# Column halves for two groups of narrow matmuls, and another order of VectorE's work in a chunk loop

## The reference, cut to what matters

```python
# prompt attention, per head and block of 128 queries, causal
sc = einsum('bqhd,bkhd->bhqk', qn, k_nope) + einsum('bqhr,bkr->bhqk', qr, k_rope)
pr = softmax(where(kpos <= qpos, sc * MLA_SCALE, -inf))
o  = einsum('bhqk,bkhd->bqhd', pr, v)                       # v has 64 columns a head

# norms: sums of squares
o_mla = rmsnorm(o_mla, g_mla_out);  m = rmsnorm(mem, g_mem_kv)
kk = kk / max(sqrt(sum(kk * kk, -1)), 1e-12)                # per head of 64

# RWKV7 recurrence, per head, state S of 64 x 64
sa = -einsum('bhvk,bhk->bhv', S, kk_t)
S  = S * d_t + sa[..., None] * (kk_t * a_t) + v_t[..., None] * k_t
y  = einsum('bhvk,bhk->bhv', S, r_t)
```

## Time and profile before

| what | us |
|---|---|
| median of 3 runs | 2296.93 (2292.48 to 3044.49) |
| profiled execution | 2297.73 |
| its span, first to last instruction | 2296.1 |
| projection | 0 to 283 |
| prompt attention | 283 to 525 |
| sample attention | 525 to 655 |
| preparation | 655 to 771 |
| chunk loop, first chunk from 771 | 771 to 1010 |
| samples' chunk | 1010 to 1085 |
| output, memory attention, feed-forward | 1085 to 2296 |

### The profile page before, as it was taken

One profiled execution on the slowest core, in us unless ns is written; L12 is line 12 of the kernel. 1 busy time (PEld: TensorE's weight loads), 2 busy tenths in 40 slices (PEclk: granted clock), 3 DMA queues, 4 the chain that ended last, 5 costly groups with the idle time before them and its releaser, 6 DMA issues. The chain is left out here.

```text
span 2296.1 us, 51205 instructions
## 1 busy us (share of the span) xinstructions
PE 2140.7 (93%) x20986; PEld 1979.9 (86%) x20986; DVE 1331.1 (58%) x2648; ACT 664.4 (29%) x1349; POOL 118.2 (5%) x194
## 2 busy tenths in 40 slices
PE   7999999997979788889999999899999999999997
PEld 6999777776769688887899879899999999999997
DVE  6356565653445456654852364366666666666676
ACT  5120244443342445541231242231122111221121
POOL 0000000004400111110000000000000000000000
PEclk9999999998978999999999999999999999999998
DMA  4111100006723100023021351111111101111112
GB/s 159 47 44 41 48 7 12 12 1 161 187 83 103 35 4 4 4 71 94 28 79 37 113 199 47 34 56 43 45 52 55 44 31 47 47 56 47 32 49 76
DMA packets 81830, 134.03 MB, mean 58 GB/s; under 512 B 27186, under 2 KB 57779, under 8 KB 81491
## 3 DMA queue, kind: packets, MB, share of 16 engines
q1 hardware_dynamic: 70482, 119.22, 16.0%
q0 software_dynamic: 4224, 8.13, 1.4%
q10 hardware_dynamic: 6912, 3.54, 0.6%
HBM read 121.58 MB, written 9.29 MB: 57 GB/s over the span
## 5 line engine op out<-in xcount | busy, mean ns | idle before, releaser
L280 PE MATMUL psum<-high,ff_up 128*128 128x352 f32 x2112 | 517.5, 326 | 7.1 <-DVE ff_up L3048 4.5
L280 PEld LDWEIGHTS psum<-high,ff_up 128*128 128x128 f32 x2112 | 371.0, 189 | 8.7 <-DVE ff_up L3048 5.2
L280 PE MATMUL psum<-low,ff_up 128*128 128x352 f32 x1056 | 341.6, 323 | 0.0
L443 PE MATMUL psum<-h_high,pj_part 128*128 128x352 f32 x960 | 242.1, 330 | 15.0 <-DVE h_low L550 14.9
L280 PE MATMUL psum<-hid,ff_down 128*128 128x352 f32 x1440 | 234.4, 324 | 0.8 <-DVE x L3109 0.8
L280 PEld LDWEIGHTS psum<-hid,ff_down 128*128 128x128 f32 x1440 | 232.8, 188 | 1.1 <-DVE x L3109 1.1
L280 PEld LDWEIGHTS psum<-low,ff_up 128*128 128x128 f32 x1056 | 199.7, 189 | 0.0
L3109 DVE TENSOR_TENSOR x<-x,psum 128x352 f32<-128x352 f32 x264 | 136.4, 521 | 105.5 <-PE psum L280 105.2
L443 PEld LDWEIGHTS psum<-h_high,pj_part 128*128 128x128 f32 x960 | 171.7, 191 | 20.6 <-issue 10.7
L2954 ACT ACTIVATE ff_up<-ff_slot 128x1024 fp32r<-128x1024 f32 x46 | 48.3, 1050 | 393.1 <-PE psum L280 384.7
L443 PE MATMUL psum<-h_low,pj_part 128*128 128x352 f32 x480 | 157.2, 328 | 0.0
(11 more groups left out here) (443 smaller groups left out, 4210.2 us busy)
## 6 DMA issues: line engine op xcount, KB each, us to landing
ff_slot<-in_w_up SPq DMA_DIRECT2D x44, 512.0 KB, 3.6
ff_slot<-in_w_down SPq DMA_DIRECT2D x22, 512.0 KB, 3.5
pj_slot<-in_w_in SPq DMA_DIRECT2D x20, 512.0 KB, 3.5
mk_slot<-in_w_mkv SPq DMA_DIRECT2D x16, 512.0 KB, 3.7
mz_k<-in_memk SPq DMA_DIRECT2D x8, 1024.0 KB, 5.7
mz_v<-in_memv SPq DMA_DIRECT2D x8, 1024.0 KB, 8.1
ms_keys<-in_lat SPq DMA_DIRECT2D x56, 128.0 KB, 3.0
ms_keys<-in_lat POOLq DMA_DIRECT2D x48, 128.0 KB, 3.0
```

The costliest lines, as they stand in the source:

```text
L280: mm = pe.matmul(ps, w(a, kk), rhs(b, kk), start=(kk == 0 and n == 0), stop=(kk == nk - 1 and n == 2))
L443: mm = pe.matmul(ps, part[:, j, a, kk * P:(kk + 1) * P], third((H, L)[b][:, kk, :], n), start=(kk == 0 and i == 0), stop=(kk == DK - 1 and ...
```

## The change

It has four parts.

1. In `values`, each matmul with 128 weight columns becomes two, one for each half of the columns: 64 weight columns each, the same stream, into the upper and the lower 64 partitions of the same area.
2. In `key_sums`, `mla_sums` and `memory_sums` the same, by a helper `halves` that gives the column ranges; the tile of 32 tokens stays in one piece.
3. In the chunk loop the plane of the values in `BK` goes, with its copy (`scaled` 0). TensorE turns the values straight from `rw`, where they lie. `bd` counts four instead of five a chunk.
4. VectorE's order in a chunk: masks, solution of chunk c - 1, `scaled` 2, `scaled` 3, states of half 0, adds of level 1, states of half 1, adds of level 2, the outputs of both halves (two copies and the add), adds of level 3, `scaled` 1, adds of level 4, `scaled` 4, adds of level 5. For the samples' chunk the order is states, states, outputs, level 1.

```diff
@@ -175,6 +175,11 @@
 
 def third(ap, n):
     return ap[:, n * C3:(n + 1) * C3]
+
+
+def halves(rows):
+
+    return [slice(lo, min(lo + HD, rows)) for lo in range(0, rows, HD)]
 
 
 class RowScale:
@@ -816,8 +821,10 @@
                     pe.wait_ge(S["t_taken"], NG * h + GSUM[i] + 2)
                     pe.wait_ge(S["o_taken"], TILES * h + i + 1)
                     for t in range(i + 1):
-                        mm = pe.matmul(B[6][:, 0:HD], pT[:, i % 2, t * P:(t + 1) * P], v[:, t, h * HD:(h + 1) * HD],
-                                       start=(t == 0), stop=(t == i))
+                        for e in range(2):
+                            rows = slice(e * HD, (e + 1) * HD)
+                            mm = pe.matmul(B[6][rows, 0:HD], pT[:, i % 2, t * P + e * HD:t * P + (e + 1) * HD],
+                                           v[:, t, h * HD:(h + 1) * HD], start=(t == 0), stop=(t == i))
                     mm.then_inc(S["o_made"], 1)
 
                 def outputs(h, g):
...
@@ -1443,8 +1449,9 @@
                         pe.wait_ge(M["root"], 1)
                     pe.wait_ge(S["sq"], q + 1)
                     for j in range(NT):
-                        mm = pe.matmul(B[6][0:rows(j), 8 * j + 2 * q:8 * j + 2 * q + 2], sq[:, q % 2, tok(j)], ends,
-                                       start=True, stop=True)
+                        for h in halves(rows(j)):
+                            mm = pe.matmul(B[6][h, 8 * j + 2 * q:8 * j + 2 * q + 2], sq[:, q % 2, j * P + h.start:j * P + h.stop], ends,
+                                           start=True, stop=True)
                     mm.then_inc(S["ss_made"], 1)
 
                 def mla_sums(i):
@@ -1452,7 +1459,9 @@
                         pe.wait_ge(M["row"], 1)
                     pe.wait_ge(S["m_squared"], i + 1)
                     for j in range(NT):
-                        mm = pe.matmul(B[3][0:rows(j), 16 * i + j:16 * i + j + 1], sq[:, i % 2, tok(j)], ones, start=True, stop=True)
+                        for h in halves(rows(j)):
+                            mm = pe.matmul(B[3][h, 16 * i + j:16 * i + j + 1], sq[:, i % 2, j * P + h.start:j * P + h.stop], ones,
+                                           start=True, stop=True)
                     mm.then_inc(S["m_sums"], 1)
 
                 def widen(ps, m, j):
@@ -1492,7 +1501,9 @@
                     pe.wait_ge(M["squared"], 1)
                     for mt in range(2):
                         for kk in range(DK):
-                            mm = pe.matmul(B[6][:, mt:mt + 1], msq[:, kk, mt * P:(mt + 1) * P], ones, start=(kk == 0), stop=(kk == DK - 1))
+                            for h in halves(P):
+                                mm = pe.matmul(B[6][h, mt:mt + 1], msq[:, kk, mt * P + h.start:mt * P + h.stop], ones,
+                                               start=(kk == 0), stop=(kk == DK - 1))
                     mm.then_inc(M["sums"], 1)
 
                 def memory_scales():
@@ -1796,7 +1807,7 @@
         prev = k.sb(ctx, "rc_prev", [P, 4, CH])
         bm = k.sb(ctx, "rc_bm", [P, NB])
         sets = [[k.sb(ctx, f"rc_{n}{e}", shape) for n, shape in (
-            ("exp", [P, 3, 4, CH]), ("KR", [P, 4, 2, CH]), ("BK", [P, 4, 3, CH]), ("A4", [P, 4, 4, CH]), ("W", [P, 4, 3, CH]),
+            ("exp", [P, 3, 4, CH]), ("KR", [P, 4, 2, CH]), ("BK", [P, 4, 2, CH]), ("A4", [P, 4, 4, CH]), ("W", [P, 4, 3, CH]),
             ("tm", [P, 4, 4, CH]), ("MV", [P, 4, CH]), ("WT", [P, 4, CH]))] for e in range(2)]
         ex_, KR_, BK_, A4_, W_, tm_, MV_t, WT_t = zip(*sets)
         SA, St, S1 = [k.at(tail, f"rc_{n}", [P, 4, CH], words=4 * CH * i) for i, n in enumerate(("SA", "S", "S1"))]
...
@@ -1842,7 +1853,8 @@
                     for hf in range(2):
                         p = 2 * hf + q
                         for i, (h, t) in enumerate(zip(HALF, tokens(c_, hf))):
-                            mm = pe.matmul(PY[hf][t, at(256 * q + 64 * j)], BK[h, p, j, :] if j < 3 else KR[h, p, 0, :], ident[i],
+                            x = BK[h, p, j, :] if j < 2 else rw[h, 8 + p, c_ * CH:(c_ + 1) * CH] if j == 2 else KR[h, p, 0, :]
+                            mm = pe.matmul(PY[hf][t, at(256 * q + 64 * j)], x, ident[i],
                                            start=True, stop=True)
                         if q and j == 3:
                             mm.then_inc(S["vt_made"], 1)
...
@@ -1948,9 +1960,7 @@
 
             tok = bass.ds(c_ * CH, CH)
             KR, BK, ex = KR_[sl], BK_[sl], ex_[sl]
-            if n == 0:
-                ins = dve.tensor_copy(BK[:, :, 2, :], rw[:, 8:12, tok])
-            elif n == 1:
+            if n == 1:
                 dve.wait_ge(S["exp"], 3 * c_ + 1)
                 ins = dve.tensor_tensor(KR[:, :, 1, :], rw[:, 0:4, tok], ex[:, 0], ALU.mult)
             elif n == 2:
@@ -1980,19 +1990,14 @@
                                          rm[:, g, 3, :].unsqueeze(1).broadcast_to([P, 2, CH]), ALU.mult, ALU.add)\
                    .then_inc(S["t_taken"], 1)
 
-        def dve_levels(dve, c_, sl, ahead=True, levels=LEVELS):
+        def dve_level(dve, c_, sl, lev):
             W = W_[sl]
-            for lev in range(1, levels):
-                for hf in range(2):
-                    pp = slice(2 * hf, 2 * hf + 2)
-                    dve.wait_ge(S["lev_made"], 12 * c_ + 2 * lev + hf + 1)
-                    dve.wait_ge(S["t_taken"], 12 * c_ + 2 * (lev - 1) + hf + 1)
-                    dve.tensor_tensor(W[:, pp, TT_, :], W[:, pp, TT_, :], two(PV[hf], 0), ALU.add)\
-                       .then_inc(S["t_taken"], 1)
-                if ahead and lev <= 4:
-                    scaled(dve, c_ + 1, 1 - sl, lev - 1)
-                    if lev == 4:
-                        scaled(dve, c_ + 1, 1 - sl, 4)
+            for hf in range(2):
+                pp = slice(2 * hf, 2 * hf + 2)
+                dve.wait_ge(S["lev_made"], 12 * c_ + 2 * lev + hf + 1)
+                dve.wait_ge(S["t_taken"], 12 * c_ + 2 * (lev - 1) + hf + 1)
+                dve.tensor_tensor(W[:, pp, TT_, :], W[:, pp, TT_, :], two(PV[hf], 0), ALU.add)\
+                   .then_inc(S["t_taken"], 1)
 
         def dve_solution(dve, c_):
             dve.wait_ge(S["sa_made"], 2 * c_ + 1)
@@ -2002,18 +2007,19 @@
             dve.wait_ge(S["sa_first"], c_ + 1)
             dve.tensor_tensor(SA[:, 2:4, :], SA[:, 2:4, :], two(PX[1], SA2_), ALU.subtract).then_inc(S["sa_taken"], 1)
 
-        def dve_state(dve, c_):
+        def dve_state(dve, c_, hf):
             dve.wait_ge(S["s1"], 4 * (c_ + 1))
+            dve.wait_ge(S["o_made"], 2 * c_ + hf + 1)
+            for q, p in enumerate(pairs(hf)):
+                dve.scalar_tensor_tensor(St[:, p, :], PU[hf][:, at(ST_ + 64 * q)], end[:, p, :], S1[:, p, :],
+                                         ALU.mult, ALU.add).then_inc(S["s_ready"], 1)
+
+        def dve_outputs(dve, c_):
             for hf in range(2):
-                dve.wait_ge(S["o_made"], 2 * c_ + hf + 1)
-                for q, p in enumerate(pairs(hf)):
-                    dve.scalar_tensor_tensor(St[:, p, :], PU[hf][:, at(ST_ + 64 * q)], end[:, p, :], S1[:, p, :],
-                                             ALU.mult, ALU.add).then_inc(S["s_ready"], 1)
                 out = c[:, 2 * hf:2 * hf + 2, bass.ds(1 + c_ * CH, CH)]
                 dve.tensor_copy(out, two(PU[hf], O_)).then_inc(S["o_first"] if hf else S["o_taken"], 1)
-                if hf:
-                    dve.wait_ge(S["o_first"], c_ + 1)
-                    dve.tensor_tensor(out, out, two(PX[hf], O2_), ALU.add).then_inc(S["o_taken"], 1)
+            dve.wait_ge(S["o_first"], c_ + 1)
+            dve.tensor_tensor(out, out, two(PX[1], O2_), ALU.add).then_inc(S["o_taken"], 1)
 
         def samples(pe, solution, outputs):
             KR, A4, W, tm, MV, WT = KR_[0], A4_[0], W_[0], tm_[0], MV_t[0], WT_t[0]
@@ -2172,8 +2178,10 @@
                 dve.tensor_tensor(sb, sb, last.unsqueeze(2).broadcast_to([P, NB, CH]), ALU.mult).then_inc(S["ns_done"], 1)
             dve_masks(dve, G, 0, 1)
             dve_solution(dve, NCH - 1)
-            dve_state(dve, NCH - 1)
-            dve_levels(dve, G, 0, False, 2)
+            dve_state(dve, NCH - 1, 0)
+            dve_state(dve, NCH - 1, 1)
+            dve_outputs(dve, NCH - 1)
+            dve_level(dve, G, 0, 1)
             fill(4)
             rest(0)
             dve.wait_ge(S["bm"], 16)
...
@@ -2332,10 +2340,23 @@
                     dve_masks(dve, c_, sl, 0)
                     if before:
                         dve_solution(dve, c_ - 1)
-                        dve_state(dve, c_ - 1)
-                    dve_levels(dve, c_, sl)
+                    scaled(dve, c_ + 1, 1 - sl, 2)
+                    scaled(dve, c_ + 1, 1 - sl, 3)
+                    if before:
+                        dve_state(dve, c_ - 1, 0)
+                    dve_level(dve, c_, sl, 1)
+                    if before:
+                        dve_state(dve, c_ - 1, 1)
```

(10 more changed lines are left out.)

7 lines of the change are left out of this document (3 added, 4 removed).

## The result

The changed kernel takes 2280.83 us (median of 5 runs, 2272.08 to 2286.57); the kernel before, run beside it, 2292.55. The ratio is 0.9943 [0.9926, 0.996]: 11.7 us less, a real gain, but a third of the 34 that I forecast. One of the five runs of before took 3044.49 us; the ratios leave out single long runs like it. The time lay inside my range, which ends at 2283, but not for the reasons that I gave, so that is luck: one term of the sum was nearly empty, and a cost that the sum doesn't have had been added elsewhere.

A forecast was written before the change was run, and what follows sets the result against it. The prediction took TensorE, 93% busy, as the bound. Values -9, preparation -11 and chunk loop -14 summed to -34 us against the profiled 2297.7, giving 2263 us, range 2246 to 2283.

The forecast's parts named there:

- the values: Prompt attention, line 819: matmuls in column halves save 10.7 us over 8 heads, less 2 for waits: -9 us (-5 to -13).
- The pair: Prompt attention: two column halves run side by side, loads too, at 0.055 us a pair against 0.107 a whole record.
- the two switches together: Prompt attention: changing tile form at either end of a group of values costs 0.15 us each, 0.30 a group.
- 2 us off for waits: Prompt attention: part of the saving only lengthens TensorE's waits for ScalarE's copy of the turned probabilities, 6.5 us before.
- the rival, loads that go one after the other: Halves' weight loads do not overlap: 2305 us, or 2383 if each half has the full 0.107; chance 0.05.
- the preparation: Sums at lines 1446, 1455, 1495: halves give -6 us, fewer low-clock dips -5; together -11 us (-4 to -16).
- The clock's part: Preparation: six low-clock dips counted behind nine bursts, 10 us in all; half taken as avoided, -5 us (0 to -10).
- the chunk loop: VectorE's new order closes TensorE's waits before level 2 and the last adds: -14 us over 15 chunks (-7 to -18).
- the 0.93 a chunk: Chunk loop: saving taken per chunk, from -0.82 at level 2, -0.30 at line 1892, and 0.07 to 0.3 of new delays.
- the 0.30: Chunk loop: one product instead of two ahead of the last adds shortens the wait of line 1892 by 0.30 us.
- The chunk loop gives nothing: Rival: VectorE's new stalls behind levels 2 and 3 eat level 2's gain; -20, 2278 us; chance 0.12.
- Switches are free: Rival: tile-form switches do not drain and the low-clock dips go; values 28 us less before waits; -50, 2247 us; chance 0.13.

The follow-up runs named there:

- interleaved: Changed kernel with jump-back hint, value halves only for groups of four or more key tiles, VectorE's other work between a level's adds: 2269.99 us, ratio 0.9884.
- thin: Changed kernel with jump-back hint, only one half of each pair in the chunk loop's first level, levels and turning, 1040 matmuls fewer, computation incomplete: 2248.25 us, ratio 0.9804.
- wait_back: Changed kernel with jump-back hint, old chunk's states and outputs back ahead of level 1's adds, scaled 2 and 3 still first: 2268.79 us, ratio 0.9885.
- chunk_only: Kernel before with only VectorE's new order in the chunk loop and the values turned from `rw`: 2295.36 us, ratio 0.999.
- values_only: Kernel before with the column halves only in the values of the prompt attention: 2285.37 us, ratio 0.996.
- sums_only: Kernel before with the column halves only in the preparation's three sums: 2283.73 us, ratio 0.9947.
- after_pad64: Changed kernel with 128 waits met at once (64 TensorE instructions) ahead of the feed-forward loop: 2277.18 us, ratio 0.9915.
- after_hint: Changed kernel with a hint ahead of the feed-forward loop's jump back: 2267.04 us, ratio 0.9864.
- before_hint: Kernel before with only the same hint ahead of the feed-forward loop's jump back: 2289.39 us, ratio 0.9981.

## Why the prediction failed, by its own steps

**Right: the values.** -9 foretold, -8.2 (alone -8.5). The pair 0.055, in fact 0.058; the two switches together 0.30, as foretold, though as 0.09 and 0.20 and not as twice 0.15; a group of one loses 0.19 (foretold 0.20) and a group of eight wins 0.56 (foretold 0.53); 2 us off for waits, in fact 2.5 on line 898. The rule of the rival, loads that go one after the other, is ruled out by 0.73 us for ten pairs. The Trainium skill's rule on row groups, in TensorE: Matmul & The Clock Gate, Part 3, thus disagrees with this trace a second time.

**Right in mechanism, one term too small: the preparation.** -11 foretold, -14.5 (alone -14.9). A burst lost 0.74 where I had 0.65. The clock's part was halved because nothing told how many dips would go. Of the six that I counted, the three behind key sums (low from 691.3, 698.1 and 704.9 us in before) and the two behind MLA sums (732.3, 745.9) are gone, and the one behind the memory's sums is half as long. With 0.74 for each of eight bursts and 1.4 for line 1495 taken off, an estimate, about -7 is left for it instead of -5.

**Wrong: the chunk loop.** -14 foretold, -2.7, alone +1.4. Over six kernels of the old order the loop takes 230.7 us on average (228.4 to 232.7), over six of the new, with interleaved, 227.8 (224.5 to 229.8): -2.9. The step that failed is not the wait: level 1 to level 2 lost 0.74 us a chunk (2.23 to 1.49, medians), where 0.82 was worked out. First, of the 0.93 a chunk 0.65 is left: without block ends the loop has 211.4 us with the old order and 201.6 with the new (means of the same kernels), 9.8 less. Level 3 takes 0.12 longer, and levels 4, 5 and the turning gain less than the 0.30 (VectorE's line 1965, up to 0.83 long, is in the way of the adds of level 4). Second, and more: the sum took the waits of TensorE for its only idle time that a change of VectorE can move, and put the time at block ends at nothing. That time went from 19.3 to 26.2 us on the same means, and 6.9 of the 9.8 were lost again; the 2.9 left are what the loop's times show. The trace of before had the sign of it: 8.0 us in 20 "issue" gaps, in a loop in which I read only the rows with a releaser. The natural reading is that a loop with fewer waits reaches the next block end sooner than the block. It fits thin, but wait_back, with the largest wait back, kept 26.2 us at the block ends; so that the closed waits had covered the fetches is not shown, only that the new order loses there most of what it gains elsewhere.

**Missed: the code's place.** A record in two halves is a load and a matmul more; the 1472 of them push every later instruction by 5.75 blocks. In the feed-forward loop this put the head eight instructions ahead of a block end: three gaps of 2.1 to 2.5 us and about 1.7 more each, with low clock behind them, about 12 us (turns of 144.6 to 145.6 us for 140.8 to 141.3). I had put the parts that the change doesn't touch at nothing. The rest as a whole is +7.3, so something gave back some 4, 3 of it in memory attention and the product behind it. The memory attention has 95.4 to 96.4 us in some kernels, before, chunk_only and after among them, and 92.3 in others (values_only, sums_only, after_pad64, wait_back, thin). Why was not isolated.

**The rivals.** "The chunk loop gives nothing" (0.12, 2278 us) was nearest to the time, by another mechanism than I gave it. "Switches are free" fell with the groups of length 1; its 28 us for the values should have been 30 by the sum's own formula (0.104 x 36 x 8). With placement out of the way, after_hint against before_hint, the change is worth 22.4 us: close to the sum with the loop at 3 in place of 14.

**Left open.** What sets when the next block is asked for, and so why one block end shows a gap and the next does not (32 of 57 in after); why the new order loses more there, when wait_back loses as much; how far the loop's spread between kernels of one order (224.5 to 229.8) is placement or chance, given one profiled execution of each; and what a loop with fewer but complete matmuls would gain, since a version that joins the level's products was not tried.

## What to carry to other kernels

Where a loop issues a small matmul every 30 ns, count its instructions as a resource: what a closed wait gains can be lost again where the next block of code is not there yet, and "issue" gaps in the profile of before are the sign. When a change adds instructions ahead of a loop, look at that loop's head in the new trace, and give the jump back its hint, before judging the change by its total. Column halves nearly halved the time of these narrow f32 matmuls, less a switch at either end of the group, so by the fit they pay beyond three key tiles a group; the shorter bursts of one- and two-column sums also gave clock back behind them.

## What was not expected of the hardware

- Steps of 0.3 to 1.8 us at every second or so of the 57 block ends in a loop of 64 x 64 f32 matmuls: 17 to 29 us at all block ends of 15 chunks, 10 with 26% fewer instructions. None of the blocks was entered less than 1.18 us behind the end of its packet.
- The feed-forward loop's jump back, over 1812 instructions, costs TensorE's sequencer 3.3 to 3.9 us, and 0.22 to 0.25 with a hint ahead of it, with which its code was not fetched again; a jump back over 377 instructions took 0.23 without one. In the two kernels whose head lay 8 and 17 instructions ahead of a block end, a second gap of 1.4 to 2.5 us followed.
- After such a gap of 2.5 us the granted clock was 0.64 over 4.6 us, an estimate of 1.7 us more (0.36 x 4.6).
- Two halves of 64 columns cost 0.058 us together, where one record of 128 costs 0.112: halves run side by side, loads and all.
